# A hybrid SSD and attention block: the attention layer streamed by token tiles and pairs of heads

## The reference

```python
# end of layer 0
x_lat = x_lat + g2 * y[:256]; x_ctx = x_ctx + cg2 * y[256:]       # y: each token's two expert rows, weighted
# layer 1
a = rms_norm(x, norm1_g) * (1 + scale) + shift                    # latent and context, each its own scale/shift
qkv = a @ w_qkv                                                   # 1024 x 1536: 16 q heads, 4 k, 4 v, of 64
q, k = rms_norm(q, q_gain), rms_norm(k, k_gain)                   # per head
q, k = apply_rope(q), apply_rope(k)                               # latent tokens only
s = einsum("bqkgd,bskd->bkgqs", q, k_all) * 64 ** -0.5
o = einsum("bkgqs,bskd->bqkgd", softmax(s), v_all)                # 4 query heads share a key head
x_lat = x_lat + g1 * (o @ w_o)
```

## Time and profile before

| | |
|---|---|
| median of three runs | 1876.92 us (1876.53 to 1877.59) |
| the profiled execution | 1877.26 us, its span 1875.4 us |
| TensorE busy | 1564.1 us, 83% |
| VectorE, ScalarE, GpSimd busy | 29%, 21%, 13% |
| DMA moved | 579.75 MB, mean 309 GB/s |
| chain that ended last | PE 46%, DMA 38%, issue 6%, DVE 5%, ACT 3% |

### The profile page before, as it was taken

The page is one execution under the profiler, slowest core; times in us unless marked ns, Lnnn a source line. Parts: engine busy times, 40 slices in busy tenths (PEclk is TensorE's granted clock), DMA queues, the critical chain, the costliest instruction groups (busy, mean ns, idle before and its releaser), DMA issues.

```text
span 1875.4 us, 21864 instructions
## 1 busy us (share of the span) xinstructions
PE 1564.1 (83%) x8778; PEld 844.7 (45%) x8778; DVE 535.4 (29%) x1057; ACT 399.2 (21%) x797; POOL 250.9 (13%) x259
## 2 busy tenths in 40 slices
PE   4999999999999889777887772939989978877774
PEld 2434445666545555343444341427555544434341
DVE  2433357777443320000000004057531000000001
ACT  2221148888400110000000003014210100000000
POOL 2000013444100111010101003010110110101001
PEclk9999999999999899999999996969989999999998
DMA  9387759995433799999999996510469999999994
GB/s 371 146 306 287 272 192 253 312 320 185 138 146 111 275 421 420 422 421 423 419 422 422 421 395 244 231 45 1 158 265 383 419 421 421 421 420 420 420 420 178
DMA packets 166141, 579.75 MB, mean 309 GB/s; under 512 B 22290, under 2 KB 77986, under 8 KB 143296
## 3 DMA queue, kind: packets, MB, share of 16 engines
q1 hardware_dynamic: 145072, 531.25, 71.7%
q0 software_dynamic: 15248, 27.62, 4.4%
q10 hardware_dynamic: 5760, 20.06, 3.2%
HBM read 550.60 MB, written 49.77 MB: 320 GB/s over the span
## 4 chain that ended last, share of the span: by engine, by line
PE 46%; DMA 38%; issue 6%; DVE 5%; ACT 3%; POOL 1%; SPq 0%; ACTq 0%; POOLq 0%; DVEq 0%
DMA mem<-in_moe_w_down_dram 34%; PE bank L531 9%; PE bank L1720 8%; PE bank L1707 6%; PE bank L880 6%; PE bank L825 3%; PE bank L330 2%; PE bank L848 2%; PE bank L2035 2%; DMA mem<-in_mod_w_dram 2%; DMA mem<-in_moe_w_gate_dram 1%; PE bank L2006 1%; ACT mem L930 1%; PE bank L1995 1%; PE bank L843 1%
## 5 line engine op out<-in xcount | busy, mean ns | idle before, releaser
L1707 PE MATMUL bank<-mem 128*64 128x256 f32 x4160 | 472.6, 381 | 86.8 <-DMA mem<-in_moe_w_up_dram 38.7
L1707 PEld LDWEIGHTS bank<-mem 128*64 128x64 f32 x4160 | 303.2, 137 | 256.2 <-DMA mem<-in_moe_w_up_dram 60.1
L1720 PE MATMUL bank<-mem 128*64 128x512 f32 x1040 | 253.9, 633 | 91.2 <-DMA mem<-in_moe_w_down_dram 82.5
L1862 DVE COPY mem<-bank 128x256 f32<-128x256 f32 x65 | 27.6, 425 | 689.3 <-PE bank L1714 689.3
L1658 POOL DMA_INDIRECT ys_dram<-mem x65 | 64.9, 998 | 863.2 <-ACT mem L1813 493.4
L1720 PEld LDWEIGHTS bank<-mem 128*64 128x64 f32 x1040 | 75.8, 144 | 227.5 <-issue 133.0
L531 PE MATMUL bank<-mem 128*128 128x512 f32 x384 | 172.3, 601 | 1.3 <-DMA mem<-in_ssd_w_in_dram 1.3
L1813 ACT ACTIVATE mem<-bank 128x512 f32<-128x512 f32 x65 | 38.8, 597 | 612.7 <-PE bank L1720 612.7
L531 PEld LDWEIGHTS bank<-mem 128*128 128x128 f32 x384 | 71.5, 191 | 99.4 <-issue 97.1
L825 PE MATMUL bank<-mem 128*128 128x512 f32 x256 | 115.2, 593 | 0.0
L880 PE MATMUL bank<-mem 128*128 128x512 f32 x256 | 112.3, 595 | 1.8 <-issue 0.9
(11 more groups left out here) (273 smaller groups left out, 1463.8 us busy)
## 6 DMA issues: line engine op xcount, KB each, us to landing
mem<-in_moe_w_up_dram SPq DMA_DIRECT2D x65, 2048.0 KB, 27.3
mem<-in_moe_w_down_dram SPq DMA_DIRECT2D x65, 2048.0 KB, 26.9
mem<-in_moe_w_gate_dram SPq DMA_DIRECT2D x65, 2048.0 KB, 26.4
mem<-in_mod_w_dram SPq DMA_DIRECT2D x24, 2048.0 KB, 8.2
ys_dram<-consts SPq DMA_DIRECT2D x54, 512.0 KB, 7.8
mem<-in_ssd_w_in_dram SPq DMA_DIRECT2D x10, 2048.0 KB, 9.3
mem<-ac_dram ACTq DMA_DIRECT2D x32, 512.0 KB, 5.5
mem<-in_ssd_w_out_dram SPq DMA_DIRECT2D x4, 2048.0 KB, 11.5
```

What stands on the lines that cost most here:

```text
L1707: mm = nc.tensor.matmul(bank[half * BR:(half + 1) * BR, 0:HF], lhsT=x[:, k], rhs=w[:, k, half * HF:(half + 1) * HF], start=(k == 0), stop= ...
L1720: mm = nc.tensor.matmul(bank[half * BR:(half + 1) * BR, :], lhsT=ht[:, k % 2, k // 2 * BR:(k // 2 + 1) * BR], rhs=w[:, k, half * COLS:(hal ...
```

## The change

- **Front.** The combination of expert rows, the norm and the turning go in two halves: tiles 0 and 1, then 2 and 3 (`stream_*`). The scaling of a tile by ScalarE is placed among the squares.
- **Projections.** The weight units come in the order first half of q, k and v, second half of q (`QKV_ORDER`). Each block is copied out, normalized and turned while TensorE multiplies the next. The query's inverse root mean square is no longer multiplied into q: it scales the exponential, and the maximum with it. Gain and rotation are one set of four tables.
- **Head loop.** Items go by pairs of heads: two tiles times two heads make four items, eight pairs. Division by the sum is now done on the probabilities before they are turned (`share`, one more VectorE instruction of 512 elements for each item); ScalarE copies the turned ones; the values product has v as its stationary side and 256 queries as its moving side, so its output needs no turning. The last block of q (tile 1, second half) is worked on inside the loop, at item 5.
- **Queue.** SP no longer waits for `cb_in` before the first qkv unit; units 6 and 7 of the second mixture wait for the last values product instead of the first output product. Rotation tables and gains are loaded at the kernel's start, the norm's columns before the first mixture.

The core of the diff:

```diff
+        QKV_ORDER = [0, 2, 1]
...
-                return qkv_mm, [2, 4, 8][n - U_QKV]
+                return qkv_mm, [2, 6, 8][n - U_QKV]
...
             elif n in (U_MOE[1] + 6, U_MOE[1] + 7):
-                sp.wait_ge(wo_mm, 1)
+                sp.wait_ge(at_pv, QH // 2)
...
+        def stream_square_act(act, t):
+            act.wait_ge(cb_x, t + 1)
+            nc.scalar.activation(xn[1][:, t, :], xin[:, t, :], ACT.Square, accum_out=ss[:, t:t + 1]).then_inc(n1_ss, 1)
+        def stream_mean_dve(dve, s):
+            dve.wait_ge(n1_ss, NT + 2 * s + 2)
+            nc.vector.tensor_scalar(ms[:, 2 * s:2 * s + 2], ss[:, 2 * s:2 * s + 2], 1.0 / D, EPS, ALU.mult,
+                                    ALU.add).then_inc(n1_ms, 1)
+        def stream_rstd_pool(pool, s):
+            pool.wait_ge(n1_ms, 2 + s)
+            nc.gpsimd.tensor_tensor(rstd[:, 2 * s:2 * s + 2], ms[:, 2 * s:2 * s + 2], mhalf[:, 0:2], ALU.pow).then_inc(
+                n1_rstd, 1)
+        def stream_rows_dve(dve, s):
+            dve.wait_ge(n1_rstd, 2 + s)
+            for t in (2 * s, 2 * s + 1):
+                nc.vector.tensor_scalar(xn[1][:, t, :], xin[:, t, :], rstd[:, t:t + 1], None, ALU.mult).then_inc(n1_xn, 1)
+        def stream_turn_pe(pe, s):
+            pe.wait_ge(n1_xn, NT + 2 * s + 2)
+            for i in range(4):
+                if s:
+                    pe.wait_ge((n1_ea, n1_ed)[i % 2], 4 + i // 2 + 1)
+                for kk in range(2):
+                    for t in range(2):
+                        c = kk * SEQ + t * P
+                        tp = nc.tensor.transpose(psum[4 + i][:, c:c + P], xn[1][:, 2 * s + t, 2 * i + kk::KD], ident)
+                tp.then_inc(n1_tp, 1)
...
+        def combine_act(act, l, t):
+            act.wait_ge(cb_in[t], 32 * (l + 1))
+            nc.scalar.activation(cy[0][:, t], cy[0][:, t], ACT.Identity, scale=r_w[:, 0, t:t + 1]).then_inc(cb_s, 1)
...
+            def values(p):
+                pe.wait_ge(at_pe, 4 * p + 4)
+                if p >= 2:
+                    pe.wait_ge(at_o, p - 1)
+                v = (KVH + p // 2) * HD
                 for k in range(NT):
+                    for hh in range(2):
+                        mm = nc.tensor.matmul(psum[4 + p % 2][HD * hh:HD * (hh + 1), 0:SEQ], lhsT=kv[:, k, v:v + HD],
+                                              rhs=probT[:, p % 2, hh, k, :], start=(k == 0), stop=(k == NT - 1),
+                                              skip_group_check=True)
...
+            pe.wait_ge(moe_out, 1)
+            stream_turn_pe(pe, 0)
+            pe.wait_ge(n1_ea, 6)
+            pe.wait_ge(n1_ed, 6)
+            unit_wait(pe, U_QKV)
+            project(0, 0, 0)
+            project(0, 1, 1)
+            stream_turn_pe(pe, 1)
+            unit_wait(pe, U_QKV + 1)
+            project(2, 0, 2)
+            project(2, 1, 3)
+            pe.wait_ge(at_qe, 2)
+            turn_q(0, 0)
+            turn_q(1, 1)
+            pe.wait_ge(n1_ea, 8)
+            pe.wait_ge(n1_ed, 8)
+            project(2, 2, 4)
+            project(2, 3, 5)
+            pe.wait_ge(at_ke, 2)
+            turn_k(0)
+            turn_k(1)
+            unit_wait(pe, U_QKV + 2)
+            project(1, 0, 6)
+            turn_k(2)
+            project(1, 1, 7)
+            turn_k(3)
+            pe.wait_ge(at_ke, 4)
+            turn_q(2, 4)
+            pe.wait_ge(at_te, 6)
+            pe.wait_ge(at_qe, 4)
             for i in range(4):
+                scores(i)
+            pe.wait_ge(at_te, 7)
+            for p in range(NPAIRS):
+                if p == 2:
+                    pe.wait_ge(at_pe, 4 * p - 1)
+                    turn_q(3, 2)
+                    pe.wait_ge(at_te, 8)
+                turn(4 * p)
+                turn(4 * p + 1)
+                if p + 1 < NPAIRS:
+                    scores(4 * p + 4)
+                    scores(4 * p + 5)
+                if p:
+                    values(p - 1)
+                turn(4 * p + 2)
+                turn(4 * p + 3)
+                if p + 1 < NPAIRS:
+                    scores(4 * p + 6)
+                    scores(4 * p + 7)
+            values(NPAIRS - 1)
...
+            for t in range(3):
+                combine_act(act, 0, t)
+            stream_square_act(act, 0)
+            stream_square_act(act, 1)
+            combine_act(act, 0, 3)
+            stream_evac_act(act, 0)
+            stream_square_act(act, 2)
+            stream_square_act(act, 3)
+            evac_q(0)
+            evac_q(1)
+            stream_evac_act(act, 1)
+            evac_kv(0)
+            evac_kv(1)
+            turned_q(0, 1, 0)
+            turned_q(1, 2, 1)
...
+            for i in range(NI2):
                 act.wait_ge(at_m, i + 1)
+                if i >= 4:
+                    act.wait_ge(at_pt, i - 3)
+                col = item_col(i)
+                nc.scalar.activation(prob[:, i % 4, :], psum[SB[i % 4]][:, :], ACT.Exp, bias=abias[:, i:i + 1],
+                                     scale=qk_rs[:, col], accum_out=asum[:, i:i + 1]).then_inc(at_p, 1)
                 if i >= 2:
+                    turned(i - 2)
+                if i == 8:
+                    turned_q(3, 8, 2)
+            turned(NI2 - 2)
+            turned(NI2 - 1)
...
+            def query(j):
+                u, t = divmod(j, 2)
+                dve.wait_ge(at_qe, j + 1)
+                x = qrow[:, t, u * COLS:(u + 1) * COLS].rearrange("p (h n) -> p h n", n=HD)
+                mean(x, 8, Q_COLS[j], 1.0 / SCALE ** 2, j // 3)
+                T = products(x, 8, qtab, t, j // 3)
+                V.tensor_tensor(x[:, :, 0::2], T[0], T[1], ALU.subtract)
+                ins = V.tensor_tensor(x[:, :, 1::2], T[2], T[3], ALU.add)
+                ins.then_inc(at_q, 1)
+                dve.wait_ge(at_q, j + 1)
+            def key(t):
+                dve.wait_ge(at_ke, t + 1)
+                x = kv[:, t, 0:KVH * HD].rearrange("p (j n) -> p j n", n=HD)
+                mean(x, KVH, K_COLS[t], 1.0)
+                dve.wait_ge(at_rs, 3 + t)
+                link(dve, V.tensor_tensor(x, x, bc(qk_rs[:, K_COLS[t]], 2, HD), ALU.mult))
+                if t < NTL:
+                    T = [bc(v, 2, 2) for v in products(x, KVH, ktab, t)]
+                    V.tensor_tensor(kdup[:, t, :, :, 0::2], T[0], T[1], ALU.subtract)
+                    ins = V.tensor_tensor(kdup[:, t, :, :, 1::2], T[2], T[3], ALU.add)
+                else:
+                    for c in range(2):
+                        ins = V.tensor_tensor(kdup[:, t, :, c, :], x, bc(kgain, 1, KVH), ALU.mult)
+                ins.then_inc(at_k, 1)
+                dve.wait_ge(at_k, t + 1)
+            def top(i):
+                dve.wait_ge(at_s, i + 1)
+                link(dve, V.tensor_reduce(amax[:, i:i + 1], psum[SB[i % 4]][:, :], AX, ALU.max))
+                V.tensor_scalar(abias[:, i:i + 1], amax[:, i:i + 1], qk_rs[:, item_col(i)], -1.0, ALU.mult,
+                                ALU.mult).then_inc(at_m, 1)
+            def share(i):
+                dve.wait_ge(at_p, i + 1)
+                link(dve, V.reciprocal(ainv[:, i:i + 1], asum[:, i:i + 1]))
+                V.tensor_scalar(prob[:, i % 4, :], prob[:, i % 4, :], ainv[:, i:i + 1], None, ALU.mult).then_inc(at_n, 1)
...
+            norm1_cols_dve(dve)
+            for t in range(2):
+                combine_rows_dve(dve, 0, t)
+                combine_add_dve(dve, 0, t)
+            stream_mean_dve(dve, 0)
+            combine_rows_dve(dve, 0, 2)
+            stream_rows_dve(dve, 0)
+            stream_evac_dve(dve, 0)
+            combine_add_dve(dve, 0, 2)
+            combine_rows_dve(dve, 0, 3)
+            combine_add_dve(dve, 0, 3)
+            stream_mean_dve(dve, 1)
+            dve.wait_ge(at_in, 48)
+            tables(qtab, qgain)
+            link(dve, tables(ktab, kgain))
+            stream_rows_dve(dve, 1)
+            query(0)
+            stream_evac_dve(dve, 1)
+            query(1)
             for t in range(NT):
+                key(t)
+            query(2)
+            dve.wait_ge(at_rs, 7)
+            top(0)
+            top(1)
+            for i in range(NI2):
+                if i == 5:
+                    query(3)
+                    dve.wait_ge(at_rs, 8)
+                if i + 2 < NI2:
+                    top(i + 2)
+                share(i)
+                if i >= 4 and i % 4 == 3:
+                    output(i // 4 - 1)
+            output(NPAIRS - 1)
...
             moe_sp(sp, 0)
-            for i in range(NT):
-                sp.wait_ge(cb_in[i], 32)
             for n in range(U_QKV, U_MOE[1]):
```

337 lines of the change are left out of this document (154 added, 183 removed).

## The result

The changed kernel takes 1884.1 us (median of 7 runs, 1879.5 to 1885.1); the kernel before took 1877.6 beside it (7 runs, 1875.2 to 1878.6). The ratio is 1.0032, with an interval of 1.0022 to 1.0042: slower, by 6.5 us, and clear of the 0.2% that can be told. 1856 was forecast, with 0.88 on faster.

The account below looks back on a forecast made before the run. The second mixture's weight stream sets the end, so the serial piece ahead of its first expert counts. A +1.7, B -29.8, C +6.8 gave -21.3, taking 1877 to 1856 us; range 1840 to 1870.

Parts of the forecast that it names:

- C: Head loop, first scores to output product: 75 us against 68.2 before, 6.8 more; bounds 64 to 80.
- the 8.2: Head loop: forecast period in us for a pair of heads (four items), against 7.5 before.
- slower: the clock: Rival, head loop: gaps drop TensorE's clock to 1.2 GHz, a pair's four items take 12 us, total 1887; chance 0.06.
- four signs of being wrong: TensorE waiting over 5 us between projections, loop period under 7.5, loop clock under 0.9, second mixture held by weights.
- its bounds: First projection at 1162.4 to 1179 for A, 62 to 68 for B, 70 to 80 for C: total 1840 to 1870.
- R: Output product to the second mixture's first expert: 50.8 us forecast, unchanged.
- fall into its idle time; if that cover fails, 2 us: Kernel's start: three more loads, 0.6 us each on GpSimd, booked at nothing, or 2 us if uncovered.
- A: Last scatter to first projection, expert-row combination and front: 1.7 us more than 37.2, first projection at 1172.6.
- The rule behind the 2.8: Gathers beside qkv weights: queues alternate by packets, so 5.9 us extra shrinks fourfold to 1.5; a gather takes 2.8.
- Gathers held at 7.2: Rival, gathers ahead of attention: each takes 7.2 us under weights, A is +8, total 1862; chance 0.20.
- weights don't disturb: Rival, gathers beside early qkv weights: no slowdown, A is -8.5, total 1846; chance 0.12.
- B: First projection to first scores: 63 us against 92.8, 29.8 less, no block late; 62 to 68 if one is.

Follow-up runs that it names:

- the gaps filled: Changed kernel with unused transposes of a constant filling TensorE's waits in the head loop; 1874.61 us, ratio 0.9980.
- the pair of runs that differ in nothing else: all four edits at 1836.24 us, against all but the loads at 1839.42 us.
- the loads moved alone: Changed kernel with the rope and gain loads moved from the start to just ahead of the router's first loads; 1877.76 us, ratio 0.9999.
- all four edits: Changed kernel, units 6 and 7 awaiting first output product, paired scores ahead of turnings, rope and gain loads behind first norm, gathered-rows wait restored; 1836.24 us.
- all but the loads: As all four edits, but with the rope and gain loads left at the kernel's start; 1839.42 us, ratio 0.9796.
- the one with the queue's part alone: Kernel before with only SyncE's wait for the gathered rows ahead of the qkv units removed; 1887.95 us, ratio 1.0043.
- the same with single scores: As all four edits, but with scores issued one item at a time ahead of each turning; 1847.47 us, ratio 0.9847.
- single scores: Changed kernel with one item's scores issued ahead of each turning in the head loop; 1864.19 us, ratio 0.9928.
- the sum of three: Changed kernel, units 6 and 7 awaiting first output product, one item's scores ahead of each turning, rope and gain loads behind first norm; 1852.32 us.
- in pairs: Changed kernel with scores issued two items at a time ahead of the two turnings instead of behind them; 1860.26 us, ratio 0.9895.

## Why the prediction was wrong

**C was mis-sized: 75 forecast, 92.8 measured.** This is the step that failed first. The text had the right order ("every second item VectorE stands still while TensorE turns, scores and drains: 1.3 us") and called the clock a rival that "sets the pace from a mean clock of 0.73 downwards". Three things in that are wrong.
- *The stand.* It is 2.68 and 1.47 per pair, 4.15 in all, against 2 x 1.3 = 2.6. The copy of the outputs, 0.42 per pair, was not in the 8.2 at all. Those two make 10.2 of the measured 10.43. At full clock the stand is 3.33, so 0.7 of the excess is a stand read too short, and 0.8 the clock.
- *The clock is no separate rival.* The text compared TensorE's whole need with VectorE's as if they lay side by side, so a clock of 0.83 would be harmless. Here they lie one behind the other: VectorE stands while TensorE turns, scores and multiplies values, so each of those counts in full at whatever clock is granted. With the gaps filled and the clock at 1.00 the loop gave back 9.0 us. By the prediction's own terms its sum turns at 10.8 us for a pair, a clock of 0.56, and not at 10.5 and 0.57.
- *The loop's start.* From the first turning, 1241.69, to that of the third pair, 1268.58, two pairs and a query take 26.9; the forecast's terms give 2 x 8.2 + 4 = 20.4. The window there has a clock of 0.59. Of the 17.8 by which C was missed, 6.5 lie in these two pairs, 1.6 ahead of the first turning and 9.7 behind.

The rival "slower: the clock", at 0.06, had 1887 and a period of 12. Its time was near, its mechanism half right: C was 93, not 106, at a mean clock of 0.83, not at the lower level throughout. The rest of the measured 1884 came from elsewhere. Of the prediction's four signs of being wrong one came true, a clock under 0.9 in the loop. The corners of its bounds add to 1872, not 1870, which changes nothing.

**R was taken at nothing: "earlier by that, never late".** Nobody asked what the two units collide with. It costs 10.6 us, shown by putting the wait back (R from 59.87 to 49.23); against the kernel before R is 9.1 longer. The prediction's own rows had the price: transfers of 512 KB under streaming weights land after 16.3 and 22.9 us. It looked there only for the gathers.

**The start: "fall into its idle time; if that cover fails, 2 us".** The cover failed. The seven kernels with the loads against the six without give 1.7 us, and the pair of runs that differ in nothing else 3 (overlapping). The remaining 2 to 3 of the 4.7 in the table arise in the first mixture, between SyncE's issues near 636 and near 679, and are not put down to the change. That stretch lasts 42.7 to 43.4 us in four of the thirteen profiles (the kernel before, the loads moved alone, all four edits, all but the loads) and 44.6 to 46.0 in the other nine, with kernels that have the loads at the start in both groups. Kernels that are the same up to there fall on both sides: the kernel before and the one with the queue's part alone (42.7 and 46.0), all four edits and the same with single scores (42.8 and 45.9). What decides it stays open. It may be why moving the loads alone showed 6 us and, in the sum of three, hardly any.

**A was right within its range, and transfers do share the engines as stated.** 38.9 forecast, 36.5 measured; 2.8 us taken per gather, 2.0 measured; 2.2 for the scatter's delay, 3.2 measured. The rule behind the 2.8, that the extra time shrinks with the packet, isn't shown: it gave 1.5 more per gather, where 0.4 to 0.6 more was measured. "Gathers held at 7.2" is out, and so is "weights don't disturb": undoing the queue's part takes 7.4 off A and gives 29.07, where 28.7 was its bound (1162.4 less 1133.7). The Trainium skill, "DMA: Bandwidth & Descriptors", section "Queues, rings and completion order", lets an engine drain a whole packet of a queue before it goes on; by the prediction's reading that meant 7.2 again, and the trace doesn't agree with that reading, at 2.0 beside qkv's 2 KB pieces. What the prediction left out is the other side: it booked the wait's price and never asked what the early issue buys. It buys nothing here, since B is 62.6 with the units issued late. In the kernel before that one edit alone costs 8 us in A.

**B was right, its last digit by luck.** 63 forecast, 62.18 measured, with no gap between projections; the sum of TensorE's rows was the answer, and VectorE kept up. Within the sum two errors cancel: transposes and six turnings took 4.4, not 6.4, what follows them 0.9, not 1.3, and the projections 56.9, not 55.2. The first 32 of their records took 15.83 us and the next 32 13.90, since the granted clock stood at 0.50 until 1178, after TensorE had been idle for 33 us ahead of the transposes. In three profiles (the loads moved alone, all four edits, all but the loads) these 32 took 13.97, and B is 60.3.

So the change's main part, the pipelined projections, brought its 30 us. Of what took them away three parts are undone by small edits: the order of scores and turnings (17 in C with single scores, 25 in pairs), the units' early wait (10.6 in R), the early qkv issue (7 in A); the loads add 2.

## What to carry to other kernels

When a loop hands work to and fro between two engines, walk one period of both queues and add what lies in series; don't take the maximum of the two needs, and count TensorE's part at the clock that its gaps will leave. A weight transfer moved earlier wasn't free in either place here: list the loads and gathers that will be in flight then, and ask who waits for them. After a large gain in one stage look at the stage behind it, where waits that were covered, and loads that were alone, now meet.

## What the runs showed of the hardware

- Scores of two items whose operands lie in different 64-row halves take 1.06 us together when both are ready at full clock, and 1.05 for one alone. The Trainium skill, "TensorEngine Tiling (Array Packing)", section "Available Configurations", lists two tiles of 64 rows by 128 columns. The trace agrees, in that two products in different halves run side by side; where the second had to wait for a semaphore they took 1.71, and 2.13 where it came 1.08 us late.
- Seven loads, 1.7 MB together, issued just behind 4 MB of weights landed in 9.2 to 15.1 us, instead of 2.8 to 5.8 in the kernel before and 2.8 to 5.7 with the weights issued behind them. The four smallest, of 128 KB and less, took 9.2 to 10.8 instead of 2.8 to 4.2.
